# Where PSUM banks are taken, softmax reciprocals are computed and the second norm's sums are added, in a two-block transformer kernel

## What is computed

```python
hx = rmsnorm(x, norm_w) * (1 + scale) + shift          # hc: the same for the context
px, pc = split_cols(hx @ w_in), split_cols(hc @ w_in)
ya, yca = global_gqa(...)                               # mixer A, rotary, q and k normed by head
yb, ycb = neighbourhood_attn(..., rpb)                  # mixer B, a bias table on the scores
yc_, ycc = window_gqa(..., sink)                        # mixer C, rotary, a sink term in the sum
ux = concatenate([ya, yb, yc_]) * silu(px[9])
x = x + gate * (ux @ w_out)                             # cx likewise, in layer 0 only
```

## Time and profile before

| | us |
|---|---|
| median of 3 runs | 1963.09 |
| lowest, highest | 1955.43, 1964.34 |
| the profiled execution, its own time | 1963.6 |
| its span, first to last instruction | 1961.7 |
| PE busy | 1882.5 (96%) |
| DVE, ACT, POOL busy | 1279.5, 1098.7, 96.9 |
| transfers | 287.42 MB, mean 147 GB/s |

### The profile page before, as it was taken

The page is one execution under the profiler, slowest core; times in us unless marked ns, Lnnn a source line. Parts: engine busy times, 40 slices in busy tenths (PEclk is TensorE's granted clock), DMA queues, the critical chain, the costliest instruction groups (busy, mean ns, idle before and its releaser), DMA issues.

```text
span 1961.7 us, 33814 instructions
## 1 busy us (share of the span) xinstructions
PE 1882.5 (96%) x13140; PEld 1630.6 (83%) x13140; DVE 1279.5 (65%) x2075; ACT 1098.7 (56%) x1915; POOL 96.9 (5%) x86
## 2 busy tenths in 40 slices
PE   6999999999899898999999999999999999999997
PEld 4977877877778787888988898889888889898886
DVE  5652354456843666876668588777776677587766
ACT  4372255274553647775456467764775555567753
POOL 2000000001200001400100010001000100010001
PEclk9999999999999999999999999999999999999999
DMA  8231242232313231455543245555555542255453
GB/s 315 87 130 65 87 150 108 86 123 72 108 67 127 80 125 66 171 192 193 211 157 109 87 172 193 192 175 190 193 181 189 215 156 100 93 189 191 175 191 148
DMA packets 42504, 287.42 MB, mean 147 GB/s; under 512 B 4928, under 2 KB 6336, under 8 KB 8848
## 3 DMA queue, kind: packets, MB, share of 16 engines
q1 hardware_dynamic: 40832, 280.33, 39.7%
q0 software_dynamic: 1552, 5.39, 0.9%
HBM read 284.65 MB, written 1.05 MB: 146 GB/s over the span
## 4 chain that ended last, share of the span: by engine, by line
issue 49%; PE 37%; DVE 6%; ACT 4%; POOL 3%; DMA 1%; SPq 0%; DVEq 0%; POOLq 0%; ACTq 0%
PE bank L2042 7%; PE bank L2044 7%; PE bank L2043 7%; PE bank L2048 6%; PE bank L2049 3%; PE bank L2219 2%; PE bank L2238 2%; PE bank L2196 2%; DVE panels_lo L1376 1%; ACT work L1011 1%; POOL work L808 1%; PE bank L2115 1%; PE bank L2230 1%; PE bank L2177 1%; POOL xT L849 1%
## 5 line engine op out<-in xcount | busy, mean ns | idle before, releaser
L1376 DVE TENSOR_TENSOR panels_lo<-raw_panels,panels_hi 128x1024 fp32r<-128x1024 f32 x472 | 581.9, 1250 | 228.8 <-ACT panels_hi L880 226.9
L2048 PE MATMUL bank<-acts,panels_hi 128*128 128x512 f32 x2032 | 717.0, 398 | 3.7 <-DVE xT L1794 1.7
L880 ACT ACTIVATE panels_hi<-raw_panels 128x1024 fp32r<-128x1024 f32 x472 | 488.5, 1054 | 298.2 <-PE bank L2044 191.4
L2049 PE MATMUL bank<-acts,panels_lo 128*128 128x256 f32 x2032 | 570.1, 281 | 0.0
L2048 PEld LDWEIGHTS bank<-acts,panels_hi 128*128 128x128 f32 x2032 | 381.4, 188 | 97.1 <-DVE xT L1794 1.9
L2049 PEld LDWEIGHTS bank<-acts,panels_lo 128*128 128x128 f32 x2032 | 383.9, 189 | 0.2
L2042 PE MATMUL bank<-acts,panels_hi 128*128 128x256 f32 (+1 forms) x984 | 302.3, 307 | 5.2 <-DVE xT L1794 1.4
L2043 PE MATMUL bank<-acts,panels_hi 128*128 128x256 f32 (+1 forms) x984 | 298.3, 303 | 0.0
L2044 PE MATMUL bank<-acts,panels_lo 128*128 128x256 f32 (+1 forms) x984 | 298.3, 303 | 0.0
L2042 PE MATMUL bank<-panels_hi,acts 128*128 128x512 f32 (+1 forms) x640 | 227.4, 355 | 8.8 <-DVE acts L1496 3.5
L2044 PE MATMUL bank<-panels_hi,acts 128*128 128x512 f32 (+1 forms) x640 | 223.6, 349 | 0.0
(11 more groups left out here) (253 smaller groups left out, 1970.9 us busy)
## 6 DMA issues: line engine op xcount, KB each, us to landing
raw_panels<-weights SPq DMA_DIRECT2D x256, 1024.0 KB, 4.8
token_major<-weights SPq DMA_DIRECT2D x4, 1024.0 KB, 12.0
near_bias<-rpb POOLq DMA_DIRECT2D x16, 256.0 KB, 3.1
xT<-xin SPq DMA_DIRECT2D x4, 512.0 KB, 5.8
gates<-weights SPq DMA_DIRECT2D x2, 1024.0 KB, 11.9
near_bias<-weights SPq DMA_DIRECT2D x2, 512.0 KB, 6.4
out<-xT SPq DMA_DIRECT2D x4, 256.0 KB, 2.2
work<-weights SPq DMA_DIRECT2D x2, 256.0 KB, 6.6
```

The source lines that it names most:

```text
L880: act.activation(slot_hi(n, a, b), raw_of(n, a, b), ACT.Copy).then_inc(hi_ready, 1)
L1376: dve.tensor_tensor(slot_lo(n, a, b), raw_of(n, a, b), slot_hi(n, a, b).bitcast(F32), ALU.subtract).then_inc(lo_ready, 1)
L2048: pe.matmul(bank.rearrange("p (c t) -> p c t", c=2), whi_, with_rest(xhi_), start=start, stop=False, skip_group_check=True)
L2049: return pe.matmul(bank[:, 0:T], wlo_, xhi_, start=False, stop=stop, skip_group_check=True)
```

## The change

Five edits to the lists of instructions; what is computed stays the same.

1. `token_half` takes a step's banks in front of its first tile: tiles 0 and 1 behind `take(s)`, tiles 2 and 3 behind `take(s + 1)`. The pairs of block 2 have two tiles and take the same step at the same place.
2. DVE's attention loop takes the reciprocals of step i-1 behind the maxima of step i, for deferred steps. Others keep their place.
3. In `wout("C")` of layer 0, DVE adds the last latents' residual in front of step 2's context residual, and ACT squares the last latents right behind the third ones.
4. POOL adds squares 0 and 1 of the latents and then their two halves; for the context it adds squares 0, 1 and 2 and the halves (6 instructions where there were 2). PE sums 1+2+2 (latents) and 1+2 (context) half squares, with two matmuls each, where it summed six of each; the latents' sums stand at three places in the last step, and the broadcast into bank 7 stands in the last step too, in front of its last `mm3`.
5. `second_norm` on DVE and ACT: both latents' scalings stand in front of the reciprocal, the low parts of tiles 0 and 1 come earlier, the last step's context residual and both context scalings later.

```diff
@@ POOL
-        for squares, ready, added in ((squares_a, sqa_ready, acca_ready), (squares_b, sqb_ready, accb_ready)):
-            pool.wait_ge(ready, 2)
-            pool.tensor_tensor(squares(0), squares(0), squares(1), ALU.add).then_inc(added, 1)
+        add_a(1, 1)
+        halves_a()
+        add_b(1, 1)
+        add_b(1, 2)
+        pool.tensor_tensor(squares_b(0)[:, 0:T], squares_b(0)[:, 0:T], squares_b(0)[:, T:2 * T], ALU.add).then_inc(accb_ready, 1)
@@ ACT, second_norm
             latents_hi(0)
             latents_hi(1)
+            latents_hi(2)
             act.wait_ge(freed, st.at["steps"] + 4)
             act.activation(tile4(squares_b(3), 2), x_pair(3, T), ACT.Square).then_inc(sqb_ready, 1)
-            latents_hi(2)
-            round_half(st.at["panels"] + 3, 0)
             latents_hi(3)
             latents_hi(4)
+            round_half(st.at["panels"] + 3, 0)
@@ ACT, wout
-                            act.wait_ge(lat_done, q + 1)
-                            act.activation(tile4(squares_a(q), 2), x_pair(q), ACT.Square).then_inc(sqa_ready, 1)
                             if q == 3:
                                 break
+                            for x in range(q, q + 1 + q // 2):
+                                act.wait_ge(lat_done, x + 1)
+                                act.activation(tile4(squares_a(x), 2), x_pair(x), ACT.Square).then_inc(sqa_ready, 1)
@@ DVE, second_norm
             scaled_c(2, 0, 3)
-            scaled_c(2, 1, st.at["steps"] + 3)
+            scaled_c(3, 0, 4)
             inverse(cstat[:, 0:4], 2).then_inc(inv_cols, 1)
-            scaled_c(3, 0, 4)
             dve.wait_ge(xl_ready, KT)
             dve.wait_ge(scale_rows, 1)
             normed(0)
             normed(1)
+            latents_lo(0)
+            normed(2)
+            latents_lo(1)
             begin(st.at["steps"] + 3)
             residual_c(3, 1).then_inc(freed, 1)
-            normed(2)
-            latents_lo(0)
+            latents_lo(2)
             normed(4)
-            latents_lo(1)
+            latents_lo(3)
             normed(6)
-            latents_lo(2)
+            latents_lo(4)
+            scaled_c(2, 1, st.at["steps"] + 3)
             scaled_c(3, 1, st.at["steps"] + 4)
-            latents_lo(3)
-            latents_lo(4)
             inverse(cstat[:, 4:8], 3).then_inc(inv_cols, 1)
@@ DVE, attention
-                if 0 <= j < len(steps) and steps[j].deferred:
-                    g, un = g0 + j, steps[j].units[0]
-                    ns = len(un.segs)
-                    dve.wait_ge(exped, now(exped, 2 * g + 2))
-                    if un.segs[0][2] is not None:
-                        dve.tensor_tensor(stat2(g, 2, ns), stat2(g, 2, ns), stat2(g, 6, ns), ALU.add).then_inc(dve_chain, 1)
-                        dve.wait_ge(dve_chain, chain.next())
-                    dve.reciprocal(stat2(g, 4, ns), stat2(g, 2, ns)).then_inc(normed, 2)
-                elif 0 <= j < len(steps):
+                if 0 <= j < len(steps) and not steps[j].deferred:
...
                     m.then_inc(negmax, 1)
+                j = i - 1
+                if 0 <= j < len(steps) and steps[j].deferred:
...
+                    dve.reciprocal(stat2(g, 4, ns), stat2(g, 2, ns)).then_inc(normed, 2)
@@ DVE, wout
                         if q == 3:
-                            dve.wait_ge(last_latents, 1)
-                            dve.wait_ge(freed, s)
-                            residual_c(3, 0).then_inc(lat_done, 1)
                             return
                         begin(s)
                         residual_c(q, 0).then_inc(lat_done, 1)
+                        if q == 2:
+                            dve.wait_ge(last_latents, 1)
+                            residual_c(3, 0).then_inc(lat_done, 1)
                         residual_c(q, 1).then_inc(freed, 1)
@@ PE, token_half (token_quarter holds the old inner loop over two feature tiles, behind its need())
             for quarter in range(2):
-                need(n, quarter)
                 for tt, bank in enumerate(banks_of):
...
+                    if half + quarter + tt % 2 == 0:
+                        take(s + tt // 2)
+                    o = token_quarter(n, half, quarter, bank, tt, blk)
@@ PE, token_sums
-                for e in range(2):
+                for e in range(2 if q else 1):
@@ PE, between the layers
-                warming(1)
-                over_rows_of_tokens(banks[7], 0)
                 over_rows_of_tokens(banks[5], 0)
@@ PE, qkv
-                        for i in range(tiles // 2):
-                            s += 1
-                            take(s)
-                        token_half(n, 0, pair, 1)
-                        token_half(n + 1, 1, pair, 1)
+                        token_half(n, 0, pair, 1, s + 1)
+                        token_half(n + 1, 1, pair, 1, s + 1)
+                        s += tiles // 2
...
-                                token_sums(banks[4], squares_b, (accb_ready, sqb_ready), (0, 2, 3), sumb_done)
+                                token_sums(banks[4], squares_b, (accb_ready, sqb_ready), (0, 3), sumb_done)
@@ PE, wout
-                                        if part + e == 2 and kt in (0, 2):
-                                            token_sums(banks[6], squares_a, (acca_ready, sqa_ready), *(((0, 2),) if kt == 0 else ((3,), suma_done)))
+                                        if (part, e, kt) == (0, 1, 0):
+                                            token_sums(banks[6], squares_a, (acca_ready, sqa_ready), (0,))
+                                        if (part, e, kt) == (1, 0, 1):
+                                            token_sums(banks[6], squares_a, (acca_ready, sqa_ready), (2,))
+                                        if (part, e, kt) == (1, 0, 3):
+                                            token_sums(banks[6], squares_a, (acca_ready, sqa_ready), (3,), suma_done)
+                                        if (part, e, kt) == (1, 1, 2):
+                                            over_rows_of_tokens(banks[7], 0)
```

More of the change, by code:

```diff
@@ L254 @@
 DVE_START2, DVE_LAYER = 182, 73
-POOL_ENTRY = 4
+POOL_ENTRY = 7
 PANELS = START2["panels"] + LAYERS * PER_LAYER["panels"]
@@ L1597, in attention @@
                     m.then_inc(negmax, 1)
+                j = i - 1
+                if 0 <= j < len(steps) and steps[j].deferred:
+                    g, un = g0 + j, steps[j].units[0]
+                    ns = len(un.segs)
+                    dve.wait_ge(exped, now(exped, 2 * g + 2))
+                    if un.segs[0][2] is not None:
+                        dve.tensor_tensor(stat2(g, 2, ns), stat2(g, 2, ns), stat2(g, 6, ns), ALU.add).then_inc(dve_chain, 1)
+                        dve.wait_ge(dve_chain, chain.next())
+                    dve.reciprocal(stat2(g, 4, ns), stat2(g, 2, ns)).then_inc(normed, 2)
                 j = i - 5
@@ L2092, in token_major, with token_quarter, token_half @@
             return o
-        def token_half(n, half, banks_of, blk):
+        def token_quarter(n, half, quarter, bank, tt, blk):
+            need(n, quarter)
+            for a in (2 * quarter, 2 * quarter + 1):
+                kt = 4 * half + a
+                xh, xl = (act_x(x, blk, kt, tt * P, (tt + 1) * P) for x in (ahi, alo))
+                o = mm3(bank[:, :], xh, xl, slot_hi(n, a * 512, a * 512 + 512), slot_lo(n, a * 512, a * 512 + 512),
+                        kt == 0, kt == KT - 1)
+            return o
+        def token_half(n, half, banks_of, blk, s, done=()):
             for quarter in range(2):
-                need(n, quarter)
                 for tt, bank in enumerate(banks_of):
-                    for a in (2 * quarter, 2 * quarter + 1):
-                        kt = 4 * half + a
-                        xh, xl = (act_x(x, blk, kt, tt * P, (tt + 1) * P) for x in (ahi, alo))
-                        o = mm3(bank[:, :], xh, xl, slot_hi(n, a * 512, a * 512 + 512), slot_lo(n, a * 512, a * 512 + 512),
-                                kt == 0, kt == KT - 1)
+                    if half + quarter == 0 and tt in done:
+                        continue
+                    if half + quarter + tt % 2 == 0:
+                        take(s + tt // 2)
+                    o = token_quarter(n, half, quarter, bank, tt, blk)
                     if half + quarter == 2 and tt + 1 < len(banks_of):
@@ L2533, in token_pair @@
                 s = st.at["steps"] + c
-                if half == 0:
-                    take(s)
-                token_half(st.at["panels"] + 2 * c + half * (2 if name == "nsa_kv" else 1), half, step_banks(s), 2)
+                token_half(st.at["panels"] + 2 * c + half * (2 if name == "nsa_kv" else 1), half, step_banks(s), 2, s)
             token_pair("nsa_q", 0, 0)
```

## The result

| | before | after |
|---|---|---|
| median of the first comparison (5 runs each) | 1956.72 | 1943.59 |
| lowest, highest | 1955.43, 1964.34 | 1940.87, 1950.76 |
| ratio, 95% interval | | 0.9922 [0.9895, 0.9949] |
| the same kernel again, beside 26 and 17 runs of before | 1959.99, 1960.26 | 0.9920 [0.9904, 0.9936], 0.9917 [0.9902, 0.9931] |
| the profiled execution, its own time and span | 1963.6, 1961.7 | 1950.76, 1948.2 |

What follows compares the result with a forecast made beforehand. TensorE bounds the kernel, busy 1882.5 of 1961.7 us, so only about 79 us of waiting could go. Terms 3.9 + 7.0 + 4.3 = 15.2 off 1963.6 gave 1948.4, forecast as 1948.5 us; range 1942.5 to 1957.

Steps and rivals of the forecast that it cites:

- Part 1: Block 2's token pairs: PE no longer waits for ACT's evictions at four places, 3.9 us less.
- Part 2: Attention loops: reciprocals behind the maxima shorten PE's waits, 7.0 us less, mostly in mixers B and C of layer 1.
- Part 3: Junction between the two layers of block 1: fewer sums and new orders, 4.3 us less.
- Start: At the junction, layer 1's first matmul comes 1.2 us earlier, with POOL's obstruction taken in.
- The case in which both of POOL's late instructions hold one: At the junction, two DVE scalings held by POOL: reciprocals 1.8 us later than covered, junction gain 2.5, time 1950.2.
- Fewer context sums: At the junction, 6 of 12 context sum matmuls in front of the fourth feature tile go, 1.5 us less.
- Clock: Behind the junction's context sums, PE's clock stays up instead of falling to half, 2.85 us less.
- Low parts met too early: At the junction, PE meets the low parts of tiles 2, 6 and 7 before they are ready, 1.2 us back.
- The junction giving little: Rival, chance 0.20: a held scaling makes reciprocals late and the clock falls anyway; junction gives 1 us, time 1951.7.
- Direct waits alone: Rival, chance 0.15: in attention ACT's copy sets the pace; the reciprocals' move gives only 2 us, time 1953.4.
- Most given back: Rival, chance 0.08: PE loses its gains at the next DVE or ACT waits; only the banks' gain stays, 1959.7.
- Slower by late reciprocals: Rival, chance 0.02: in attention PE's broadcasts wait for moved reciprocals, 39 us lost, time 1987.

Runs made afterwards that it cites:

- reciprocals alone: Kernel before with only DVE's reciprocals of step i-1 moved behind the maxima of step i; ratio to before 0.9969.
- banks alone: Kernel before with only the order in which a token pair takes its banks changed; ratio to before 0.9979.
- sums only: Kernel before with squares summed as in the changed kernel, six context sum matmuls, and every order left old; ratio to before 0.9987.
- twelve sums: Changed kernel with the context's sums as before, 12 matmuls, POOL adding only squares 0 and 1 for them; ratio to before 0.9949.
- both_filled: Changed kernel with ACT's high parts 6 and 7 and panel roundings earlier, plus matmuls computing nothing before layer 1's third scores and first key transposes; ratio 0.9920.

## Why the prediction was right, and where not

**Sum and sign: right.** 15.2 us forecast, 15 to 16 measured in three comparisons. The absolute forecast, 1948.5, was built on a profiled execution at 1963.6; more runs of before gave medians of 1956.7, 1960.0, 1959.0 and 1960.3. So 1943.6 was measured, near the lower end of the range of 1942.5 to 1957, with about the forecast gain. Two or three executions don't fix a level to 5 us.

**Part 1: right.** 3.9 forecast, 1.01 at each of four places, 4.1 timed, no new wait.

**Part 2: mechanism right, size too large** (7.0 against 5.2 in the trace and 6.1 timed). The step that failed is "0.4, 0.4 and 0.3", 1.1 in sum, for the tails of layer 0: in the profile of the reciprocals alone its three stages changed by 0.09 or less, and no other profile has a gain there. I had written that ACT sets these ends and then took the wait on DVE's multiply as a gain all the same. In the changed kernel the 0.42 of the earlier trace rows is gone, and PE waits 0.38 for ACT's copy (line 1000) at 142.46 instead. B and C came to 3.0 and 2.2 for 3.4 and 2.5: with the reciprocals alone PE still waits 0.46 for DVE's multiply at 655.14 in B, and of the waits on ACT's copies in C the 0.52 at 736.83 before shrank only to 0.19 (729.30), a 0.52 further on (744.75) stayed whole.

**Part 3: the sum right, 4.3 against 4.0 to 4.5, its terms not quite.** Start: 1.2 forecast, 1.6 measured; I had taken one held scaling in, and none was. The case in which both of POOL's late instructions hold one (1950.2), which the Trainium skill (SBUF — State Buffer, Who interferes with whom) would make the rule where the two engines' instructions interleave, did not come up: all four scalings had begun before POOL, the last by 0.11 us, so that this price was not paid is in part luck. The prediction's "four new instructions" on POOL are three. Fewer context sums: 1.5 forecast, 2.74 against 1.40, 1.3. Clock: 2.85 forecast; from the first matmul to the split it is 11.38 with both halves of the stretch and 9.41 in the profile of the banks alone, whose stretch came earlier, so 2.0: part of the slow time fell into idle time of PE. Low parts met too early: 1.2 forecast, 0.5 measured (8.52 from first matmul to split with the new order, 8.06 with sums only). With these sizes the sum is 1.6 + 1.3 + 2.0 - 0.5 = 4.4, beside 4.5 between the two first profiles: errors of both signs met. That DVE's chain carries it to the keys was right to 0.1 in every profile (34.0 us from the split to the keys in all eleven with ACT's old order).

**What was not foreseen** is that the clock gives and takes elsewhere. In the first profile of the changed kernel a stretch in mixer C's tail of layer 0 took 2.2 us, those at 637 and 719 took 1.5 of the 3.0 and 0.8 of the 2.2. The forecast spoke of the clock only at the junction.

**The rivals.** The junction giving little: no. Direct waits alone: no, B gave 3.0. Most given back: no, the parts add up. Slower by late reciprocals: no, a whole iteration later cost about 1 us in the trace. The prediction had read the slack from one row, 5.2 us; over the 68 reciprocals of the kernel before the shortest was 3.0, still over the 2.1 that it asked for.

## What to carry to other kernels

An order of instructions is worth changing where an engine's next wait is for something it could have done before; the gain ends at the engine that is next, so follow the chain to it by rows before adding up waits, and take nothing at a place whose end another engine sets. A sum by a float32 matmul with two columns cost 0.23 us here, as much as an fp32r one with 512 columns; let an idle engine add first. For parts of 0.2% read the distance between the same two instructions in two traces, not the median.

## What the runs showed of the hardware

**The clock.** Every stretch at a granted share of 0.50, 1.2 GHz, lasted 3.41, 6.83 or 10.24 us, the one at the end of each span aside. In front of the junction's stretches PE had never idled long: 1.48 at 480.73 before (the stretch begins at 485.4), 0.79 at 474.18 with twelve sums (480.4), and with the banks alone not at all in the 22.2 us ahead of it:

```profile
449.70:471.90 22.20, 22.20 (x131) 19.73 (x131) 13.49 (x30) 7.81 (x11) 2.75 (x2) 1.00 0.26 95
471.90:475.30 3.40, 3.40 (x15) 3.22 (x15) 0.93 (x4) 0.26 (x1) 0.00 (x0) 0.50 0.01 2
```

All four profiles with twelve context sums have such a stretch, none of the ten with six has (nine of them with the new order too, sums only with the old one). The Trainium skill (TensorE: Matmul & The Clock Gate, HAM oscillation) describes the fall as coming from waits between groups of matmuls; here it came without a long wait, at runs of matmuls with two columns. That these bring it fits all 14 profiles, but no run changes them with POOL's additions left as they were. At the ramps of layer 1's three attention stages 9 of 12 profiles without fillers have a stretch in at least one, neither of the two with them has.

**Two paces of the same loop.** In block 2 the same 956 matmuls of one stage took 165.78 us from first to last start in six of the 14 profiles and 168.96 in eight, those of a later one of the same form 165.78 or 168.96 (seven each), and those of one between them 168.96 in all, at a granted clock of 1.00. No edit goes with it: the changed kernel's profiles have both. Eleven pairs of matmuls of the first stage in the changed kernel's third profile and in the last one with fillers (both_filled):

```profile
1199.87 0.39 PE L2052 MATMUL bank<-acts,panels_hi 128*128 128x512 f32 x1
...
1203.68 0.40 PE L2052 MATMUL bank<-acts,panels_hi 128*128 128x512 f32 x1
```

```profile
1199.69 0.40 PE L2052 MATMUL bank<-acts,panels_hi 128*128 128x512 f32 x1
...
1203.58 0.40 PE L2052 MATMUL bank<-acts,panels_hi 128*128 128x512 f32 x1
```

3.81 and 3.89 us, a pair 346 and 354 ns, throughout the stage. What picks the pace is open. Two such stages at 3.2 us, the start with up to 3.7 and stretches at half clock (1.6 where PE is the bound, as the one at 1021 before) can make up the 12.5 us by which 26 executions of before differ; that is an estimate, since only one execution of each comparison has a trace.
